# A Mamba mixer in a two-layer decoder step: projection, chunk scan and gating interleaved by group

## The reference

```python
z, xbc, dt_raw = jnp.split(u @ w_in, [D_INNER, D_INNER + CONV_DIM], axis=-1)      # 2048, 4096, 32 columns
xbc_full = jnp.concatenate([conv0, xbc], axis=1)
conv = conv_b + sum(xbc_full[:, k:k + t_len] * conv_w[k] for k in range(4))
xs, bm, cm = jnp.split(silu(conv), [2048, 3072], axis=-1)       # 32 heads of 64; 8 groups of 128 states
dt = softplus(dt_raw + dt_bias); a = -exp(a_log)
y, h_last = ssd_scan(xs, dt, a, bm, cm, ssm0)                   # two chunks of 128 tokens, state carried
y = y + d_skip[:, None] * xs
gated = y * silu(z)
gg = gated by group; gg = gg * rsqrt(mean(gg * gg, axis=-1) + EPS)    # 8 groups of 256
out = (gg * norm_g) @ w_out
```

## Time and profile before

| what | us |
|---|---|
| median of three runs (1402.08 to 1407.09) | 1404.25 |
| profiled execution, its own time | 1412.56 |
| its span | 1410.7 |
| PE busy | 1318.6 |
| DVE busy | 947.0 |
| ACT busy | 670.5 |
| POOL busy | 162.2 |

### The profile page before, as it was taken

One profiled execution on the slowest core, in us unless ns is written; L12 is line 12 of the kernel. 1 busy time (PEld: TensorE's weight loads), 2 busy tenths in 40 slices (PEclk: granted clock), 3 DMA queues, 4 the chain that ended last, 5 costly groups with the idle time before them and its releaser, 6 DMA issues.

```text
span 1410.7 us, 27171 instructions
## 1 busy us (share of the span) xinstructions
PE 1318.6 (93%) x9958; PEld 1250.7 (89%) x9958; DVE 947.0 (67%) x1565; ACT 670.5 (48%) x1064; POOL 162.2 (11%) x148
## 2 busy tenths in 40 slices
PE   5999997996999759999999989999997999999998
PEld 5999997996998639999999889999974789999997
DVE  6666449999336774766767977774476647666547
ACT  5444345554124643655545665553441436444335
POOL 2000002001000000022247222210010001000001
PEclk9999999997689869999999999999996579999999
DMA  8555555444322117457769545575531004555552
GB/s 300 185 179 178 179 179 224 158 157 129 135 88 77 38 42 264 159 181 272 270 243 352 201 178 210 178 289 188 179 120 38 1 31 160 189 180 178 174 181 79
DMA packets 60969, 237.89 MB, mean 169 GB/s; under 512 B 7000, under 2 KB 8184, under 8 KB 56392
## 3 DMA queue, kind: packets, MB, share of 16 engines
q1 hardware_dynamic: 54864, 197.01, 40.0%
q0 software_dynamic: 5760, 39.57, 7.8%
q10 hardware_dynamic: 288, 0.54, 0.1%
HBM read 225.79 MB, written 13.39 MB: 170 GB/s over the span
## 4 chain that ended last, share of the span: by engine, by line
PE 73%; DVE 15%; ACT 4%; issue 4%; POOL 2%; DMA 1%; DVEq 1%; ACTq 0%; SPq 0%; POOLq 0%
PE bank L360 21%; PE bank L361 20%; PE bank L362 20%; DVE wlo L1058 4%; DVE xact L1277 3%; PE bank L583 2%; DVE xl L1077 1%; ACT whi L736 1%; DVE x L1088 1%; PE bank L695 1%; PE bank L688 1%; POOL sq L1595 1%; PE bank L687 1%; PE bank L433 1%; DVE gu L1104 1%
## 5 line engine op out<-in xcount | busy, mean ns | idle before, releaser
L1058 DVE TENSOR_TENSOR wlo<-raw,whi 128x1024 fp32r<-128x1024 f32 x369 | 485.3, 1319 | 267.4 <-ACT whi L736 265.5
L360 PE MATMUL bank<-xh,whi 128*128 128x264 f32 x2024 | 594.5, 294 | 31.0 <-DVE xl L1077 14.7
L361 PE MATMUL bank<-xl,whi 128*128 128x264 f32 x2024 | 582.0, 288 | 0.0
L362 PE MATMUL bank<-xh,wlo 128*128 128x264 f32 x2024 | 581.2, 287 | 0.0
L736 ACT ACTIVATE whi<-raw 128x1024 fp32r<-128x1024 f32 x369 | 388.0, 1054 | 329.8 <-PE bank L362 318.2
L360 PEld LDWEIGHTS bank<-xh,whi 128*128 128x128 f32 x2024 | 390.5, 193 | 45.5 <-issue 22.3
L361 PEld LDWEIGHTS bank<-xl,whi 128*128 128x128 f32 x2024 | 390.5, 193 | 0.9
L362 PEld LDWEIGHTS bank<-xh,wlo 128*128 128x128 f32 x2024 | 388.3, 192 | 0.0
L360 PE MATMUL bank<-hh,whi 128*128 (+1 forms) x896 | 255.8, 286 | 1.0 <-ACT xact L971 0.6
L362 PE MATMUL bank<-hh,wlo 128*128 (+1 forms) x896 | 255.8, 285 | 0.0
L361 PE MATMUL bank<-hl,whi 128*128 (+1 forms) x896 | 255.0, 285 | 0.0
(11 more groups left out here) (269 smaller groups left out, 1150.8 us busy)
## 6 DMA issues: line engine op xcount, KB each, us to landing
raw<-weights SPq DMA_DIRECT2D x369, 512.0 KB, 3.2
h<-ssm POOLq DMA_DIRECT2D x8, 1024.0 KB, 6.6
xact<-ssm POOLq DMA_DIRECT2D x8, 1024.0 KB, 6.1
out_ssm_s<-xact POOLq DMA_DIRECT2D x8, 1024.0 KB, 5.9
xact<-dtx_rows POOLq DMA_DIRECT2D x5, 1024.0 KB, 9.2
zs<-dtx_rows POOLq DMA_DIRECT2D x3, 1024.0 KB, 9.6
x<-xT SPq DMA_DIRECT2D x1, 1056.0 KB, 5.5
out_y<-x SPq DMA_DIRECT2D x8, 132.0 KB, 1.8
```

Source lines behind the costliest of these rows:

```text
L360: pe.matmul(out, whi[:, w, c], rh, start=start, stop=False)
L361: pe.matmul(out, whi[:, w, c], rl, start=False, stop=False)
L362: return pe.matmul(out, wlo[:, w, c], rh, start=False, stop=stop)
L1058: dve.tensor_tensor(wlo[:, s, :], raw[:, s, :], whi[:, s, :].bitcast(F32), ALU.subtract).then_inc(lo_ready, 1)
```

## The change

The units of `sin` are put in another order: dt, then for each group its four conv tiles followed by one or more z tiles. The loops are unrolled into 53 slots; slots 0 to 48 begin with a unit. `CHUNK_AT`, `DEC_AT`, `GATE_AT`, `NORM_AT`, `ROOT_AT` and `APPLY_AT` say in which slot the other work of a group stands. From unit 4 on all units of the stage use two PSUM banks.

- dt is computed on 128 partitions x 66 columns (`dt_take`), in pieces over slots 0 to 3. The weight of dt was already repeated four times.
- A take writes 264 columns into `xraw`. POOL copies the last 11 (three of the tail, eight of decode) into `tailraw`, and the take of the tile four later waits for that copy (`tail_copied`).
- The decode convolution, products and outputs go group by group to POOL (`dec_conv`, `dec_products`, `dec_outputs`), with a silu on ACT (`dec_silu`) and two ops on DVE (`decode_read`).
- The decode states are stored by group instead of by sequence. `decode_state(g)` forms 16 products for 8 sequences and two tiles, plus one with `ones`. Three buffers take the place of four, and they and other scratch lie in the space of `hh` and `hl`.
- Norm sums of four groups go into the four 32-row quadrants of bank 2. One root (ACT) and one reciprocal (DVE) serve four groups; the rows go through DRAM (`stat_rows`) and come back broadcast.
- The first eight tiles are scaled and split in slots 42 to 50, the last eight under the first units of `sout`.
- dt x is transposed once, as 128 x 128, behind the fourth unit of `f2i0`. The late work goes by group: its broadcast has rows of 1 KB, 40 pieces stand before `pg0` instead of 48, and `late_unit` is new.

The core of the diff:

```diff
+Z_AFTER = {0: [0], 1: [1], 2: [2], 3: [3, 4], 4: [5, 6], 5: [7, 8], 6: [9, 10], 7: [11, 12, 13, 14, 15]}
+SIN = [("dt", 0)]
+for _g in range(G):
+    SIN += [("conv", 4 * _g + _k) for _k in range(4)] + [("z", _t) for _t in Z_AFTER[_g]]
+CHUNK_AT = [10, 14, 18, 22, 28, 34, 40, 46]
+DEC_CONV_AT = [e_ + 1 for e_ in LAST_CONV]
+DEC_SILU_AT = [e_ + 2 for e_ in LAST_CONV]
+DEC_PROD_AT = [10] + [e_ + 3 for e_ in LAST_CONV[1:]]
+DEC_AT = [13, 17, 21, 25, 31, 37, 43, 47]
+GATE_AT = [15, 22, 28, 34, 40, 46, 48, 50]
+NORM_AT = [t_ + 1 for t_ in GATE_AT]
+ROOT_AT = [NORM_AT[3] + 1, NORM_AT[7] + 1]
+APPLY_AT = 42
+SLOTS = ROOT_AT[1] + 1
...
-    if n < 20:
-        return U0["f2i0"] + 4 + 2 * n
-    if n < 48:
-        return U0["f2o0"] + 3 * (n - 20) // 4
-    return U0["f1i1"] + 4 + 2 * (n - 48)
+    if n < 17:
+        return U0["f2i0"] + 10 + 2 * n
+    if n < 40:
+        return U0["pp0"] + n - 17
+    return U0["f1i1"] + 4 + 5 * (n - 40) // 3
...
+            def decode_state(g):
...
+                for q in range(SEQS):
+                    for t in range(2):
+                        pe.matmul(bank[2][:, c_ + 8 * t + q:c_ + 8 * t + q + 1], h0_[:, 256 * q + 128 * t:256 * q + 128 * t + 128],
+                                  dact[:, g, 1, q:q + 1], start=True, stop=True)
+                pe.matmul(bank[2][:, c_ + 16:c_ + 24], ones, bc_d[:, g, :], start=True, stop=True).then_inc(h0_used, 1)
...
+                rows = bank[2][32 * (g % 4):32 * (g % 4) + 32, 0:N]
+                pe.matmul(rows, ones[:, 0:32], gsq[:, 0, :], start=True, stop=False)
+                pe.matmul(rows, ones[:, 0:32], gsq[:, 1, :], start=False, stop=True).then_inc(gated_sum, 1)
...
+            def pre_tokens():
+
+                pe.wait_ge(dt_d_step, DT_STEPS)
+                pe.transpose(bank[4][:, 0:64], dd[:, 0:128], ident[0:64, 0:64])
...
+            for s_ in range(SLOTS):
+                if s_ < len(SIN):
+                    sin_unit(s_)
+                if s_ == 4:
+                    pre_tokens()
+                if s_ == 6:
+                    pre_sums()
+                for g in range(G):
+                    if s_ == CHUNK_AT[g] + 3:
+                        add_inter(g)
+                for g in range(G):
+                    if s_ == CHUNK_AT[g]:
+                        chunk_in(2 * g)
+                    if s_ == CHUNK_AT[g] + 1:
+                        chunk_in(2 * g + 1)
+                        chunk_out(2 * g)
+                    if s_ == CHUNK_AT[g] + 2:
+                        chunk_out(2 * g + 1)
                 if s_ in NORM_AT:
                     norm_sums(NORM_AT.index(s_))
+                if s_ in DEC_AT:
+                    decode_state(DEC_AT.index(s_))
+            pe.wait_ge(ssd_y, G)
+            pe.wait_ge(gated_std, 2)
             stage_b("sout", XT, "f2i0")
-            ffn_in("f2i0", 1)
+            ffn_in("f2i0", 1, dtx_rows_out)
...
+            def conv_in(s_, c):
+
+                if c >= 4:
+                    dve.wait_ge(tail_copied, c - 3)
+                take(xraw[:, c % 4, 3:3 + N], "sin", s_, banks=sin_banks(s_))
...
+            invert_stats(1)
+            for j in range(XT - 2):
+                ahead("sout", 0, j)
+                if 2 <= j < 6:
+                    if j == 2:
+                        dve.wait_ge(stat_in, 32)
+                    for t in (2 * j + 4, 2 * j + 5):
+                        normed(t)
...
+            def tail_copy(s_, c):
+
+                pool.wait_ge(a_free, A0["sin"] + s_ + 1 + 4)
+                pool.tensor_copy(tailraw[:, c, :], xraw[:, c % 4, T:T + 3 + SEQS]).then_inc(tail_copied, 1)
...
+            def stats_in(b):
+
+                pool.wait_ge(stat_out, 16 * (b + 1))
+                pool.dma_start(xact[:, 8 * b:8 * b + 8:2, :], stat_rows[4 * b:4 * b + 4, :].unsqueeze(0).to_broadcast([P, 4, N])).then_inc(stat_in, 16)
```

More of the change, by code:

```diff
@@ L587, in norm_sums @@
             def norm_sums(g):
                 pe.wait_ge(gated_sq, g + 1)
[L590 to L593, removed]
+                pe.wait_ge(dec_read, [d_ < NORM_AT[g] for d_ in DEC_AT].count(True))
+                if g >= 4:
+                    pe.wait_ge(gated_std, 1)
@@ L596, in _, with dtx_rows_out @@
+            def dtx_rows_out():
+                pe.wait_ge(b_free, 8 * 1 + 6)
+                pe.wait_ge(dec_prod, G)
+                pe.transpose(bank[5][:, 0:P], dtx_d[:, :, :].rearrange("p k s -> p (k s)"), ident).then_inc(dtx_tr, 1)
             ffn_in("f1i0", None)
             stage_b("f1o0", FT, "sin")
[L598 to L604, removed]
@@ L607, in _ @@
[L607 to L615, removed]
@@ new lines, in _ @@
+            for s_ in range(SLOTS):
+                kind, i = SIN[s_] if s_ < len(SIN) else ("", 0)
+                last, li = SIN[s_ - 1] if 0 < s_ <= len(SIN) else ("", 0)
+                if kind == "dt":
+                    ahead("sin", 0, 0)
+                    row_factor("sin")
+                    dt_take()
+                if kind == "conv":
+                    conv_in(s_, i)
+                if kind == "z":
+                    z_take(s_, i)
+                if s_ - 1 in DEC_AT:
+                    decode_read(DEC_AT.index(s_ - 1))
+                if last == "conv":
+                    conv_taps(li)
+                if 0 < s_ < len(SIN):
+                    ahead("sin", 0, s_)
+                if s_ == 1:
+                    dt_start()
+                if s_ == 2:
+                    dt_series((15, 13, 11, 9))
+                if s_ == 3:
+                    dt_series((7, 5, 3))
+                    dt_end()
+                if s_ == 5:
+                    pre_tokens()
+                if s_ == 7:
+                    pre_sums()
+                if s_ == 8:
+                    pre_diff(0)
+                if s_ == 9:
+                    pre_diff(1)
+                    pre_decode()
+                if s_ in GATE_AT:
+                    gate(GATE_AT.index(s_))
+                for g in range(G):
+                    if s_ == CHUNK_AT[g] + 3:
+                        finish(g)
+                for g in range(G):
+                    if s_ == CHUNK_AT[g]:
+                        chunk_in(2 * g)
+                        decay(2 * g)
+                    if s_ == CHUNK_AT[g] + 1:
+                        chunk_in(2 * g + 1)
+                        decay(2 * g + 1)
+                        carry(2 * g)
+                    if s_ == CHUNK_AT[g] + 2:
+                        carry(2 * g + 1)
+                if s_ - 1 == ROOT_AT[0]:
+                    invert_stats(0)
+                if 0 <= s_ - APPLY_AT < 8:
+                    if s_ == APPLY_AT:
+                        dve.wait_ge(stat_in, 16)
+                        dve.wait_ge(h0_used, 6)
+                    normed(s_ - APPLY_AT)
+                if 0 <= s_ - APPLY_AT - 1 < 8:
+                    low_z(s_ - APPLY_AT - 1)
```

687 lines of the change are left out of this document (354 added, 333 removed).

## The result

The changed kernel takes 1430.28 us (median of four, 1417.34 to 1432.4) against 1405.67; the ratio is 1.016, 95% interval 1.009 to 1.023. I had forecast 1366.5 within 1345 to 1390. It is slower, outside the range, on the side to which I gave 4%; whether by more than 2% the interval leaves open. All ratios here are of fast executions; a slow one of `e1_wide_rows`, 2443.81 us beside nine of 1385.6 to 1398.5, is not in them.

A forecast was written before the change was run, and what follows sets the result against it. TensorE bounds the kernel, except in the mixer, where it waits for DVE. T0 270.5 + work 185.4 + clock 14.4 + waits 13.4 + tail 6.9 put `sout` at 490.6, 37.7 us earlier: 1366.5 us, range 1345 to 1390.

The forecast's parts named there:

- Late work: Behind the mixer: 40 pieces before `pg0` instead of 48, POOL waiting there for TensorE; no cost, within 2 us either way.
- E: Rival: POOL becomes the bound, DVE standing when POOL is four tiles late; 1406 to 1415 us, chance 0.04.
- The mixer's gain: Mixer's projection and scan: interleaving lets `sout` start at 490.6 instead of 528.3, 37.7 us gained.
- T0: Mixer start, slots 0 to 10: select and difference of chunk 0 end at 270.5; the start gives nothing.
- Work at full clock: PE's work from T0 to the last chunk, units, chunks, decode and norm sums: 185.4 us.
- Clock: Mixer groups: half clock behind each of 8 decodes costs 1.8 us, 14.4 in all, between 0 and 8 x 2.9.
- Waits: Mixer groups: PE bounds each group and only latency stays, 13.4 us over eight groups, between 0 and 4 each.
- Tail: From the last chunk's output to `sout`: add_inter, norm sum, gate, root and others with hand-overs, 6.9 us.
- B: Rival: mixer waits and clock loss mostly vanish because dense units surround every decode; 1339 to 1352 us, chance 0.17.
- C: Rival: DVE becomes the bound in the mixer, stretched by POOL's small ops; 1380 to 1400 us, chance 0.18.
- D: Rival: ACT's table switches drain, each group's first exp 1.4 us later, 11 us more; 1377.5 us, chance 0.03.
- F: Rival: PE waits at the start and group edges until nothing is left; 1400 to 1408 us, chance 0.03.

The follow-up runs named there:

- e1_wide_rows: The changed kernel with dt x laid out in DRAM so each partition's 8 KB are one piece instead of eight of 1 KB: 1393.08 us, ratio 0.988.
- Experiments 1 and 2: 1 is e1_wide_rows; 2 is the kernel before with only its dt x broadcast cut into eight 1 KB pieces per partition: 1453.61 us, ratio 1.035.
- experiment 7: e1_wide_rows with the last 24 late pieces every 4/3 unit instead of every 5/3, ending 8 units earlier: 1388.42 us, ratio 0.984.
- experiments 5 and 6: 5: changed kernel, 16 one-column decode products replaced by two of 8 columns, 1389.37 us (one execution); 6: e1_wide_rows, decode states in two halves, 1376.26 us.
- e9_halves_and_late: e1_wide_rows with decode states in halves (group 5's whole) and the last late pieces every 4/3 unit: 1367.58 us, ratio 0.972.

## Why the prediction was wrong, point by point

**The step that failed** is the last term, "Late work. ... POOL waits there for TensorE, which runs at 2.9 a unit: no cost, within 2 us either way", and with it the tail's sentence that its write and the first late loads "have six units (17 us)". I gave the new broadcast no time of its own; the only landing that I used for one was the old one's 9.2 us. The change cuts each partition's 8 KB into eight pieces; that landed in 19.5 and 27.1 us (medians) and starved the weight ring. In place of "within 2 us" 38.5 us were lost between `sout` and the head norms. Experiments 1 and 2 show it from both sides: +46 us when only this is put into the kernel before, -37 us when it is taken out of the changed one (with the order in which ACT and POOL read the buffer). I had listed the rows of 1 KB and asked only when the buffer is needed, not what the transfer does to the queue that everything hangs on. The same term missed a smaller cost, the 6 us of the pieces' places (experiment 7). No rival had either; E was on the right side with another mechanism.

The pieces are not the whole miss. `e1_wide_rows` without them measured 1393.08, still 3 us above the range. Its profiled span is 17.7 us shorter than the one before instead of 37.7: 13.4 are missing at `sout` (503.97 instead of 490.6) and 6.3 behind it.

**The mixer's gain** was the right mechanism and 11.3 us too large (`sout` 490.6 forecast, 501.87 measured). By terms:
- T0 (start): 270.5 forecast, 271.56 measured, with the gap of 11.2 us at 230 ended by DVE (ten forecast). The sum is better than its parts: dt's chain ended at 241.1 instead of 239.5, and a conv unit cost DVE 2.92 us (230.84 to 233.76) instead of 3.12.
- Work at full clock: 185.4 forecast, 211.18 - 19.0 = 192.2 measured, 6.8 more. I gave all 38 units 2.90; a unit that starts or ends beside short matmuls takes 3.0 to 3.1 (291.81 to 294.81 is one).
- Clock: 14.4 forecast, 19.0 measured here and 23.8 in `e1_wide_rows` with the same mixer. That one-column products bring the half level was right (experiments 5 and 6), the 1.8 us for each too small.
- Waits: 13.4 forecast, 222.34 - 211.18 = 11.2 measured. In five of the groups the second chunk's difference waits 1.15 us for the exponential.
- Tail: 6.9 forecast, 8.0 measured.

**Rivals.** B (clock and waits vanish) does not come with the change as it is, but most of its clock half can be had: with halves 6.0 us are lost. C (DVE stretched by POOL) is refuted for the groups by `wlo` between 272 and 494 in the changed kernel, min, median and max ns:

```profile
L1122 DVE TENSOR_TENSOR wlo<-raw,whi x39: 1211/1221/1278, 274.5 to 493.4; 128x1024 fp32r<-128x1024 f32 x39
```

The short POOL ops, a copy mostly 0.4 us, do not lengthen it; the 2.34 us of the earlier trace rows stood beside POOL's squares. D (a drain behind the table load): the changed kernel's timeline of ACT has the load and the work behind it as in the earlier trace rows, with no second piece:

```profile
264.33 1.28 ACT L1011 ACT_TABLE_LOAD   x1
265.63 0.36 ACT L1011 ACTIVATE tok<-tok 128x192 f32<-128x192 f32 x1
```

E (POOL as bound): POOL is busy 33.75 us in the 222 of the groups, and no wait of DVE there is ended by POOL. F (nothing left) fell with the mixer's 26.4 us.

**What stays open.** Why the granted clock of the attention layer differed between the two profiles (0.91 and 0.89); what sets the exact price of pieces between 1 and 2 KB, and whether it is their length or that they lie apart in DRAM (8 KB from one to the next with 1 KB pieces, 16 KB with 2 KB ones), since no run cuts a row whose pieces adjoin; and whether the start can give anything, since in both tries DVE's chain came as late as before. A version without the broadcasts was not tried.

## What to carry to other kernels

When a buffer changes its index order, look at each DMA that reads or writes it and ask how long the contiguous pieces are now: the bytes and the KB of the issue line stay the same while the transfer takes twice the time of all 16 engines. A transfer that nobody waits for can still delay the stream that everybody waits for; hold the landing time of the stream's own loads under it against the time that their ring covers (here 11.6 us: loads of 4.5 us cost nearly nothing, those of 14.8 stopped PE). And where thin matmuls stand in a long row, try them in small portions between dense ones: here that gave 15.8 us.

## What was not expected of the hardware

- A broadcast of 1 MB to 128 partitions landed in 9.2 us in pieces of 8 KB, 12.6 in 2 KB, 18.4 in 1 KB, with 5760, 6800 and 6800 packets in the queue over the whole kernel.
- In the changed kernel five of the eight decode states (16 one-column products in a row, 3.63 us at full clock) were followed by a unit that began at 1.2 GHz, 0.42 us a matmul; in a sixth the clock fell inside that unit, and behind the first two it did not fall. In `e1_wide_rows` all eight units began at 1.2 GHz. In halves (1.84 us) with a unit between them only group 5's did, behind the wait of 2.71 us. Total work was equal, and 15.8 us came back at `sout` (503.97 less 490.49 is 13.5, and the start was 2.3 later). In `e9_halves_and_late` the clock fell once more behind halves (group 7, at 472.4), so the length of the row alone does not decide.
- With the same mixer, the same stretch lost 19.0 and 23.8 us to the clock in two executions; differences under 5 us there mean nothing from one profile.
